# Where two of four softmax exponentials stand in ScalarE's order, in a one-core encoder block

## What is computed

```
h = rmsnorm(x);  proj = h @ w_in             # q|k|v of A, q|k|v|z|a|b of B, gates ga|gb
ya = swa_sink_attention(aq, ak, av)          # 8 heads, window of 128 keys, a learned sink
yb = gated_deltanet(bq, bk, bv, bz, ba, bb)
x = x + (sigmoid(ga) * (ya @ w_up_a) + sigmoid(gb) * (yb @ w_up_b)) @ w_out
x = x + memory_cross_attention(rmsnorm(x), rmsnorm(mem))
x = x + hierarchical_moe(rmsnorm(x))         # 32 experts, top 2 in the top group
out = rmsnorm(x)
```

```
m = maximum(max(scores), sink);  p = exp(scores - m)
probs = p / (sum(p) + exp(sink - m));  o = probs @ v
```

## Time and profile before

| | us |
|---|---|
| median of 3 runs | 874.52 (874.24 to 875.8) |
| the profiled execution | 871.63 |
| its span, first to last instruction | 869.8 |
| TensorE busy in the span | 789.8 (91%) |
| VectorE, ScalarE, GpSimd busy | 352.6, 241.3, 292.4 |

### The profile page before, as it was taken

One profiled execution on the slowest core, in us unless ns is written; L12 is line 12 of the kernel. 1 busy time (PEld: TensorE's weight loads), 2 busy tenths in 40 slices (PEclk: granted clock), 3 DMA queues, 4 the chain that ended last, 5 costly groups with the idle time before them and its releaser, 6 DMA issues.

```text
span 869.8 us, 14886 instructions
## 1 busy us (share of the span) xinstructions
PE 789.8 (91%) x5813; PEld 642.5 (74%) x5813; DVE 352.6 (41%) x756; ACT 241.3 (28%) x418; POOL 292.4 (34%) x263
## 2 busy tenths in 40 slices
PE   5999999899899979999996998998999999987783
PEld 5888798788788857688885877887777777765551
DVE  5388760572663771336612612363222222221115
ACT  5333242112311756522211545330111111110102
POOL 3723444422430343043352245252333333332110
PEclk9999999999999998999999899999999999999997
DMA  9855504202210350455485272648999999999946
GB/s 247 157 100 108 113 9 98 49 1 50 49 40 11 68 126 2 96 139 153 97 224 114 50 242 96 254 179 311 363 390 383 391 393 389 388 385 384 396 182 257
DMA packets 73230, 162.77 MB, mean 187 GB/s; under 512 B 18834, under 2 KB 46306, under 8 KB 65240
## 3 DMA queue, kind: packets, MB, share of 16 engines
q1 hardware_dynamic: 65712, 150.66, 54.9%
q0 software_dynamic: 5472, 9.82, 3.4%
q10 hardware_dynamic: 1992, 1.55, 0.9%
HBM read 157.31 MB, written 13.04 MB: 196 GB/s over the span
## 4 chain that ended last, share of the span: by engine, by line
PE 56%; DMA 26%; DVE 7%; issue 5%; ACT 3%; POOL 2%; SPq 1%; POOLq 0%; DVEq 0%; ACTq 0%
PE bank L1019 15%; DMA arena<-in_w_exp_up 14%; PE bank L1026 11%; PE bank L1028 11%; PE bank L1027 11%; DMA ring<-in_w_exp_up 8%; PE bank L1363 3%; DMA ring<-in_w_cq 1%; PE bank L1373 1%; DMA hT<-h_rows,rt 1%; DVE arena L1755 1%; PE bank L1229 1%; PE bank L1320 1%; ACT w_high L1438 1%; DMA arena<-y_half 1%
## 5 line engine op out<-in xcount | busy, mean ns | idle before, releaser
L1026 PE MATMUL bank<-h_hi,w_high 128*128 128x512 f32 x296 | 123.2, 416 | 2.3 <-DVEq L561 2.0
L839 POOL TENSOR_TENSOR ring_low<-ring,w_high 128x2048 fp32r<-128x2048 f32 (+1 forms) x16 | 71.5, 4467 | 149.6 <-ACT w_high L1438 133.0
L1363 PEld LDWEIGHTS bank<-arena,hT 128*64 128x64 f32 x1728 | 98.3, 138 | 25.6 <-issue 22.8
L1027 PE MATMUL bank<-h_lo,w_high 128*128 128x512 f32 x296 | 116.5, 394 | 0.0
L1363 PE MATMUL bank<-arena,hT 128*64 128x128 f32 x1728 | 102.3, 276 | 8.6 <-DMA arena<-in_w_exp_up 7.7
L839 POOL TENSOR_TENSOR w_low<-ring,w_high 128x2048 fp32r<-128x2048 f32 x14 | 64.3, 4596 | 80.0 <-ACT w_high L1438 79.9
L2025 DVE SCALAR_TENSOR_TENSOR rt<-rt,bank 128x128 f32<-128x128 f32 x32 | 9.2, 288 | 176.4 <-ACT rt L1650 176.4
L1438 ACT ACTIVATE w_high<-ring 128x2048 fp32r<-128x2048 f32 (+1 forms) x32 | 58.8, 1838 | 68.4 <-PE bank L1028 31.0
L1026 PEld LDWEIGHTS bank<-h_hi,w_high 128*128 128x128 f32 x296 | 56.3, 190 | 15.2 <-DVEq L561 2.3
L1028 PE MATMUL bank<-h_hi,ring_low 128*128 128x512 f32 x168 | 66.7, 397 | 0.0
L1027 PEld LDWEIGHTS bank<-h_lo,w_high 128*128 128x128 f32 x296 | 56.2, 190 | 9.7
(11 more groups left out here) (312 smaller groups left out, 1408.4 us busy)
## 6 DMA issues: line engine op xcount, KB each, us to landing
arena<-in_w_exp_gate SPq DMA_DIRECT2D x27, 1024.0 KB
arena<-in_w_exp_up SPq DMA_DIRECT2D x27, 1024.0 KB
arena<-in_w_exp_down SPq DMA_DIRECT2D x27, 1024.0 KB
ring<-in_w_in SPq DMA_DIRECT2D x33, 512.0 KB, 6.7
ring<-in_w_exp_gate SPq DMA_DIRECT2D x5, 1024.0 KB
ring<-in_w_exp_up SPq DMA_DIRECT2D x5, 1024.0 KB
ring<-in_w_exp_down SPq DMA_DIRECT2D x5, 1024.0 KB
xres<-in_x SPq DMA_DIRECT2D x8, 512.0 KB, 7.4
```

What stands on the lines that cost most here:

```text
L839: after(pool.tensor_tensor(low, full, high, ALU.subtract), w_lo)
L1026: pe.matmul(o, l_hi, r_hi, start=(n == 0), stop=False)
L1027: pe.matmul(o, l_hi, r_lo, start=False, stop=False)
L1363: ins = pe.matmul(bank[CAP * half:CAP * half + CAP, 1, P * n:P * n + P], xgT[:, x, kk, :], w[:, kk, P * half:P * half + P], start=(kk == 0 ...
```

## The change

A table names the job at which ScalarE takes each tile's exponentials. Tiles 0 and 1 stay at the job they had. Tile 2 moves from `("sc", 2, 3)` to `("sc", 3, 0)`, behind ScalarE's share of `("gb", 3)`, `("pv", 0)` and `("pt", 1, 0..3)`. Tile 3 moves from `("sc", 3, 3)` to `("pt", 2, 3)`, behind the weight chunk's rounding, `("gb", 4)`, `("ty", 0..3)`, `("pv", 1)` and `("pt", 2, 0..2)`, and ahead of the copy of `("pt", 2, 3)`. No instruction is added or removed, and the lists of the other engines stay as they are.

```diff
+EXP_AT = {("sc", 0, 3): 0, ("sc", 1, 3): 1, ("sc", 3, 0): 2, ("pt", 2, 3): 3}
 SOFTMAX_AT = {("gb", 1): 0, ("sc", 2, 0): 1, ("sc", 3, 0): 2, ("gb", 5): 3}
...
-                if k == "sc" and c == 3:
-                    s = scores_of(job[1])
-                    act.wait_ge(sub_ready, job[1] + 1)
-                    stat, sums8 = stat2[:, job[1] % 2], sums2[:, job[1] % 2]
+                if job in EXP_AT:
+                    t = EXP_AT[job]
+                    s = scores_of(t)
+                    act.wait_ge(sub_ready, t + 1)
+                    stat, sums8 = stat2[:, t % 2], sums2[:, t % 2]
                     for h in range(A_HEADS):
                         after(nc.scalar.activation(s[:, h], s[:, h], ACT.Exp, bias=stat[:, 8 + h:9 + h], accum_out=sums8[:, h:h + 1]))
                     after(nc.scalar.activation(stat[:, 0:8], stat[:, 0:8], ACT.Exp), p_exp)
```

## The result

The changed kernel takes 869.61 us in the median (869.48 to 871.18), measured beside 875.16 us (874.24 to 876.32) for the kernel before: ratio 0.9944, 95% interval 0.9927 to 0.9961, or 4.9 us less; the two medians themselves lie 5.6 us apart. Forecast were 867.8 us, 6.76 us less. Two later measurements of the same kernel gave 0.9935 (0.9912 to 0.9957) and 0.9919 (0.9900 to 0.9938), with medians 6.8 and 7.6 us apart. Four executions of the later measurements, one of them of the kernel before, took 1008 us or more and are left out of all ratios. The profiled execution took 869.48 us with a span of 867.7 us.

What follows compares the result with a forecast made beforehand. TensorE's own program was taken to bound the first 594 us, a weight stream the rest. Terms 5.34 + 1.67 - 0.25 = 6.76 us gave 867.8 us from 874.52 (-0.77%), own range 866.3 to 869.3.

Steps and rivals of the forecast that it cites:

- The place of the gain: TensorE's 4.34 us wait from 321.18 us, for ScalarE copies standing behind tile 2's exponentials only by order, would go.
- Term 1: At tile 3's scores: without the wait and the slow second half, ("gb",4) begins 5.34 us earlier.
- Term 2: At ("gb",4): if the clock stays at 1.00, it takes 5.75 in place of 7.42 us, a gain of 1.67 us.
- Rival B: Before ("gb",4) the clock falls all the same; gain only about 4.2 to 5.1 us, 869.4 to 870.3 us; chance 0.12.
- rival A: Whole kernel: the full gain as worked out, 867.8 us, own range 866.3 to 869.3; chance 0.70.
- Term 3: At ("pv",2): it waits for the copy behind tile 3's delayed exponentials, 0.25 us lost, bounds 0 and 0.8.
- The sum at ("pv",2): 5.34 + 1.67 - 0.25 = 6.76 us; ("pv",2) starts at 340.1 in place of 346.87 us.
- A shift to the end: Behind ("pv",2) everything just moves earlier, the experts' stage by 6.8 us and as long as before.
- rival C: Further on the gain is given back, by slow clock or weight stream: 874.5 us, or 871 to 874 in part; chance 0.13.
- a sign of its own: At 594 us: the prediction is wrong if the shift at 347 us is not found there.
- The profiled execution and the median: Whole kernel: profiled 871.63 us, median 874.52, 2.9 us above; the change should act on both alike, giving 864.9 and 867.8.
- Rival D: At ("pv",2): slower, a long wait for the copy behind the exponentials makes the clock fall; chance 0.05.

## Why the prediction was right

1. **The place of the gain** was right. The wait for the copies behind tile 2's exponentials was the loss, and it is gone. The trial of each move alone shows a thing that the prediction doesn't have: tile 2's move needs tile 3's. With tile 3's exponentials left at ("sc",3,3), the emptying of ("gb",4) stands behind them and the wait is 6.59 us. The prediction gave tile 3's move a cost alone; in truth it is a condition of the whole gain.
2. **Term 1**, 5.34 us: from the scores of tile 2 to ("gb",4) it was 19.66 us and is 323.46 - 309.15 = 14.31: 5.35.
3. **Term 2**, the clock, 1.67 us: ("gb",4) took 7.42 and takes 5.64 us, 1.78. Rival B is refuted by the windows, 1.00 over the transposes, and not by the time: 869.61 lies just above rival A's own range (866.3 to 869.3) and within rival B's (869.4 to 870.3), so the number alone would have pointed to the wrong one. The page of the Trainium skill named there (TensorE: Matmul & The Clock Gate, Part 4: PE-mode transpose) would have transposes not engage the full clock. The stretch doesn't bear that out, but it doesn't test it either, since its longest run of transposes alone is the 1.8 us from 329.10. Nor is a long wait the only thing behind a fall: in the changed kernel's first trace the clock falls at 577.9 us with TensorE busy since 575.15, behind a wait of 0.58 us and matmuls of 36 and 64 columns. No run here explains that fall.
4. **Term 3**, 0.25 us: 0.28, 0.23 and 0.28 in three traces. Its mechanism was right too: VectorE's step was held for 3.31 us (forecast 3), until GpSimd's instruction ended, and the hold moved to tile 2's step when that instruction was moved. The rule of the Trainium skill (SBUF — State Buffer, Who interferes with whom) is borne out in that VectorE is held, for 1.75 to 4.5 us in these traces; that GpSimd is held in its turn, no run here shows.
5. **The sum at ("pv",2)**, 6.76 us: 6.79 against the first trace, 6.51 against the second, where the clock came back a little sooner.
6. **A shift to the end.** This is where the number lies off, and rival C is what to test. By a sign of its own the prediction fails in the first pair of traces: the experts' loop, promised 6.8 us earlier, issues its first load at 598.48 us where the kernel before had 597.58. Counted from the scores of tile 2 that is 289.3 against 290.1 us, so 0.8 us were left. The later traces have 296.2 before, and 283.2 and 284.1 in the changed kernel: the difference comes and goes with the long form of the half clock, 17 us in place of 3.4, for which the prediction left 1.5 us either way in rival A's range. From ("pv",2) to the last prefetch the two traces of before take 242.68 and 242.69 us, the three of the changed kernel 242.25, 242.35 and 241.64: nothing is lost. To the end of the span it is 522.9 and 526.7 before, 525.9, 524.0 and 522.5 after: means of 524.8 and 524.1. So the traces show no systematic loss, only a scatter of 4 us that both kernels have. Most of it goes with how long the clock stays low shortly before the experts' stage: over all twelve traces of this document the remainder is 525.9 to 526.8 us in the three with the long form and 521.5 to 524.0 in the other nine. The three ratios, 4.9, 5.7 and 7.1 us, lie around 6.65 / 875 = 0.76%, two of them below it, and the medians, 5.6, 6.8 and 7.6 us apart, lie evenly around it. That the first measurement came out low, and how near it came to the forecast all the same, is chance as far as these runs tell. A loss of up to about a microsecond behind 347 us can't be excluded by times.
7. **The profiled execution and the median.** The prediction scaled one to the other by 2.9 us; the first profiled execution of before (871.63) was the quickest of its kernel on record, and the changed kernel's (869.48) was at its median. The two spans alone, 869.8 and 867.7, would have told a third of the gain.
8. **Slips without effect on the sum.** The chunk's rounding moved by ten microseconds (335.85 to 325.9) and not by eight. Rival D's price of a wait, 4.34 us and 2.4 us of slow matmuls, is by the prediction's own terms 7.01 - 4.34 = 2.67 us beside the wait.

## What to carry to other kernels

When an engine empties another's buffers in a fixed order, a long step that needs late data should stand behind the copies that are already due, up to the slack of whoever reads its result. Moving one such step often only hands the wait on: look at what is emptied next, and move the next long step with it. Judge a change of this size by a stretch measured start to start in several traces, since the rest of a long program scatters by as much as the change is worth.

## What the runs showed of the hardware

- A VectorE instruction of 0.17 us with two operands in SBUF lasted 1.75, 3.29, 3.31, 3.86 and 4.33 us when it met a GpSimd subtraction on SBUF that had begun earlier, each time until within 0.04 us of its end. One with a single SBUF operand, the maximum over 1536 columns, kept its 1.75 us with GpSimd at work (330.59 us above).
- In this stretch TensorE's clock fell during the long waits and not during the short one. With a wait of 3.0 us it was half for 3.4 us in all, with 4.3 us for 6.8 us, the end of the wait included; over one of 1.6 us it kept the full clock. Against the 32.34 us of a stretch with the old wait alone, the waits of 3.0, 4.34 and 6.59 us cost 4.4, 7.1 and 8.2 us.
- The clock also falls with TensorE busy, at 577.9 us above behind a wait of only 0.58 us. Near that place one and the same program ran at half clock for 3.4, 6.8 or 17 us in different executions. From the last prefetch to the first load of the experts' loop it is then 8.0 to 8.4, 9.6 to 9.8 or 14.4 us, and with the long form the remainder behind ("pv",2) takes 2 to 5 us longer.
